# One split, one chain and one decay block in another order, and a second buffer for the end-decay exponent, in the HGRN2 mixer of a two-block model

## The reference, cut to what matters

```python
def hgrn2_scan(q, k, v, logf, s0, with_output):
    ...
    kc, vc = chunks(k), chunks(v)
    gcum = jnp.cumsum(chunks(logf), axis=2)
    g_end = gcum[:, :, -1]
    k_end = kc * jnp.exp(g_end[:, :, None] - gcum)
    chunk_states = jnp.einsum("bcshk,bcshv->bchkv", k_end, vc)
    s_final, s_in = lax.scan(_carry_step, s0, (jnp.moveaxis(jnp.exp(g_end)[..., None], 1, 0),
                                               jnp.moveaxis(chunk_states, 1, 0)))
    ...
    q_rel = qc * jnp.exp(gcum - g_mid)
    k_rel = kc * jnp.exp(g_mid - gcum)
    att = jnp.where(causal, jnp.einsum("bclhk,bcshk->bchls", q_rel, k_rel), 0.0)
    o_intra = jnp.einsum("bchls,bcshv->bclhv", att, vc)
    o_inter = jnp.einsum("bclhk,bchkv->bclhv", qc * jnp.exp(gcum), s_in)
    return (o_intra + o_inter).reshape(bsz, seqlen, nh, dv), s_final
```

## Time and profile before

| what | value |
|---|---|
| median of three runs | 2863.11 us |
| profiled execution, its own time | 2866.0 us |
| its span | 2863.2 us |
| PE busy | 2325.6 us (81%) |
| DVE busy | 1724.7 us (60%) |
| ACT busy | 1282.8 us (45%) |
| rounds 1 and 2 and what leads in, 2163 to 2224 us | 61.0 us |
| rounds 3 to 8, 2224 to 2388 us | 164.0 us |

### The profile page before, as it was taken

How to read it: one execution, slowest core, us unless ns; L and a number is a source line. 1 busy time by engine, 2 the same in 40 slices (tenths; PEclk the granted TensorE clock), 3 DMA queues, 4 the chain that set the end, 5 groups by cost and what they waited for, 6 DMA issues and landing times. The chain is left out here.

```text
span 2863.2 us, 36429 instructions
## 1 busy us (share of the span) xinstructions
PE 2325.6 (81%) x11964; PEld 1845.0 (64%) x11964; DVE 1724.7 (60%) x2894; ACT 1282.8 (45%) x1924; POOL 254.2 (9%) x329
## 2 busy tenths in 40 slices
PE   4999799899878787776766977999658886689994
PEld 3989666789841565655663446778547776577783
DVE  4773425376310348997884026999645877379994
ACT  2663125365210345543112025888536663168883
POOL 0000000000000055652000000111100000001100
PEclk8999899899999798987887987999879898789997
DMA  5344321344359421210000216999812111289992
GB/s 190 147 170 150 119 95 38 114 165 162 122 220 409 163 67 59 66 55 20 1 1 0 74 73 220 390 389 391 312 52 82 60 59 45 75 310 396 395 395 102
DMA packets 126952, 454.75 MB, mean 159 GB/s; under 512 B 13792, under 2 KB 17504, under 8 KB 126688
## 3 DMA queue, kind: packets, MB, share of 16 engines
q1 hardware_dynamic: 115872, 413.15, 38.9%
q0 software_dynamic: 10944, 39.85, 3.7%
HBM read 431.97 MB, written 20.97 MB: 158 GB/s over the span
## 5 line engine op out<-in xcount | busy, mean ns | idle before, releaser
L2136 DVE TENSOR_TENSOR moe_w_lo<-ring,moe_w_hi 128x1024 fp32r<-128x1024 f32 x384 | 462.5, 1221 | 62.3 <-ACT moe_w_hi L2074 57.2
L2074 ACT CAST moe_w_hi<-ring 128x1024 fp32r<-128x1024 f32 x384 | 399.2, 1049 | 147.4 <-PE ps L252 119.6
L250 PE MATMUL ps<-ffn_h_hi,ffn_w_hi 128*128 128x256 f32 x704 | 205.4, 292 | 33.0 <-DVE ffn_h_lo L369 17.3
L250 PE MATMUL ps<-moe_w_hi,moe_own 128*128 128x512 f32 x512 | 213.9, 418 | 12.0 <-DVE moe_own L2143 11.1
L251 PE MATMUL ps<-moe_w_lo,moe_own 128*128 128x512 f32 x512 | 205.0, 400 | 0.0
L252 PE MATMUL ps<-moe_w_hi,moe_own 128*128 128x512 f32 x512 | 204.8, 400 | 0.0
L251 PE MATMUL ps<-ffn_h_lo,ffn_w_hi 128*128 128x256 f32 x704 | 202.1, 287 | 0.0
L252 PE MATMUL ps<-ffn_h_hi,ffn_w_lo 128*128 128x256 f32 x704 | 202.0, 287 | 0.0
L250 PE MATMUL ps<-even_h_hi,even_w_hi 128*128 128x512 f32 x320 | 140.0, 438 | 74.9 <-DVE even_w_lo L1403 74.7
L359 DVE TENSOR_TENSOR ffn_w_lo<-ring,ffn_w_hi 128x1024 fp32r<-128x1024 f32 x132 | 155.3, 1218 | 68.4 <-ACT ffn_w_hi L326 68.4
L326 ACT CAST ffn_w_hi<-ring 128x1024 fp32r<-128x1024 f32 x132 | 131.3, 1046 | 125.7 <-PE ps L252 69.0
(11 more groups left out here) (426 smaller groups left out, 5468.7 us busy)
## 6 DMA issues: line engine op xcount, KB each, us to landing
ring<-in_weights SPq DMA_DIRECT2D x766, 512.0 KB, 5.7
expert_rows<-moe_y POOLq DMA_DIRECT2D x32, 512.0 KB, 7.2
token_rows<-moe_token_rows SPq DMA_DIRECT2D x6, 512.0 KB, 2.6
sq<-in_cmp_w SPq DMA_DIRECT2D x1, 2048.0 KB, 7.9
both<-in_x SPq DMA_DIRECT2D x1, 1024.0 KB, 5.9
both<-in_context SPq DMA_DIRECT2D x1, 1024.0 KB, 8.2
out<-both SPq DMA_DIRECT2D x1, 1024.0 KB, 4.8
cols<-in_cols SPq DMA_DIRECT2D x1, 724.5 KB, 9.3
```

Of the source, the lines that this page charges most:

```text
L250: pe.matmul(out, w_hi, x_hi, start=start, stop=False)
L2074: act.copy(w_hi[:, j % WB].rearrange("p h f -> p (h f)"), k.slot(act, first + GU + j, e).rearrange("p a f -> p (a f)")).then_inc(w_rounded, 1)
L2136: dve.tensor_tensor(w_lo[:, j % WB].rearrange("p h f -> p (h f)"), k.ring[:, (first + GU + j) % RING].rearrange("p a f -> p (a f)"), w_hi[ ...
```

## The change

In `exps` the first exponential reads `ke[:, d, :]` and not `logs[:, d, :]`, and in `decays` the difference "end of chunk minus running sum" is written into `ke[:, d, :]`. Since PE's transposes of the head before read `ke`, `decays` waits for them (`turned`, from head 1 on). On ACT, the cast at place 0 stands ahead of `exps(h-1,0)`. On DVE, `chain(h-2,0)` stands behind the split at place 0, and `decays(h-1,1)` behind that chain.

```diff
@@ exps
-                        act.activation(ke[:, d, :], logs[:, d, :], ACT.Exp)
+                        act.activation(ke[:, d, :], ke[:, d, :], ACT.Exp)
@@ ACT, for h in range(ROUNDS)
                         if live(h - 2):
                             keep_turned(h - 2, 0)
+                        for n in places[0]:
+                            split(n + WB)
                         if live(h - 1):
                             exps(h - 1, 0)
-                        for n in places[0]:
-                            split(n + WB)
                         if live(h - 2):
                             keep_turned(h - 2, 1)
@@ decays
+                        if h:
+                            dve.wait_ge(turned, u - 1)
                         if d == 0:
-                            dve.tensor_tensor(L.rearrange("p (c t) -> p c t", t=GC), end, chunks, ALU.subtract)
+                            dve.tensor_tensor(ke[:, d, :].rearrange("p (c t) -> p c t", t=GC), end, chunks, ALU.subtract)
                             mid, edge = HC // 2 - 1, HC - 1
                         else:
-                            dve.tensor_tensor(L, gg[:, :], L, ALU.subtract)
+                            dve.tensor_tensor(ke[:, d, :], gg[:, :], L, ALU.subtract)
                             dve.drain()
-                            dve.tensor_tensor(chunks, end, L.rearrange("p (c t) -> p c t", t=GC), ALU.subtract)
+                            dve.tensor_tensor(chunks, end, ke[:, d, :].rearrange("p (c t) -> p c t", t=GC), ALU.subtract)
@@ DVE, for h in range(ROUNDS)
                         if live(h - 1):
                             decays(h - 1, 0)
-                            decays(h - 1, 1)
                         if live(h - 2):
                             mask(h - 2, 0)
-                            chain(h - 2, 0)
                         for n in places[0]:
                             split(n + WB)
+                        if live(h - 2):
+                            chain(h - 2, 0)
                         if live(h - 1):
+                            decays(h - 1, 1)
                             weigh(h - 1, 0)
```

## The result

| what | before | after |
|---|---|---|
| median, first comparison (4 runs each) | 2861.27 us | 2883.85 us |
| its ratio, 95% interval | | 1.0078, 1.0052 to 1.0102 |
| repeat, later (23 and 6 runs) | 2867.01 us | 2884.33 us |
| its ratio, 95% interval | | 1.0064, 1.0051 to 1.0078 |
| span of the profiled execution | 2863.2 us | 2880.8 us |

The changed kernel is slower, as forecast, but by more: 22.6 us in the first comparison, 17.3 in the repeat, 13.7 forecast. 2883.85 us lies above the range (2867 to 2882).

What follows compares the result with a forecast made beforehand. The bound was a loop: PE from mix to attend 1, then 9.64 us over ACT and DVE to the next mix. Waits of 11.3 plus 2.4 of clock gave 13.7 us: 2876.8 us from 2863.1, range 2867 to 2882.

Steps and rivals of the forecast that it cites:

- The chain in rounds 3 to 7: DVE's cast-split-chain-decays row starts direction 1's exponential at C + 9.47 against C + 8.21: 1.26 us later a round, 6.3 in all.
- Round 8: Two tiles at place 0, attend 1 early: direction 1's exponential moves from C + 5.60 to C + 9.47, 3.87 us of delay.
- C: The start of carry 0 on PE in a round, from which the prediction counts the other starts; 2288.74 in round 5.
- Rounds 1 and 2: In round 1 a split stands ahead of the decays that `exps(0,1)` waits for; 1.14 us together, through to round 3's mix.
- Edits at nothing: Transposes' wait, direction 0's exponentials behind the cast, writing `ke`, the first exponential in place and SyncE's queue: costed at 0.
- The wait for the transposes: In round 5 DVE stands 0.7 us before decays 0 writes `ke`; idleness before the split covers it, so cost 0.
- The clock: PE's halved clock after idle gaps, from mix to C: 0 to 4.8 us more with longer gaps, half taken, 2.4.
- rival 3: The clock drop falls into the longer idle gap and is over when the mix begins: -3.1 us, 2860 us; chance 0.04.
- Rival 1: Every gap costs the full clock price, round 9's mix too: 8.0 us of clock, total 19.3, 2882 us; chance 0.20.
- Rival 2: In rounds 3 to 7 the slow clock reaches past C, attend 1 is late and hides the delay: 2868 to 2870.5 us; chance 0.11.
- Rival 4: The place 0 split no longer stands between chain 0 and `weigh`, freeing the chain: 2863 us, no change; chance 0.05.

Runs made afterwards that it cites:

- the parts: The change's three parts, each alone against the kernel before: ACT's order, ratio 1.0009; the buffer and its wait, 1.0010; DVE's order, 1.0086.
- the filled kernels: Kernel before and changed kernel with 10 and 15 overwritten matmuls in PE's gaps before the mix: ratios 0.9949 and 0.9982 to the unfilled kernel before.

## Why the prediction was right in its mechanism and wrong in its size

1. *The chain in rounds 3 to 7.* Right: 1.29 us a round against 1.26, link by link, and the exponential changed its releaser. By the parts, DVE's order makes it, not the cast and not the buffer.
2. *Round 8.* Right: 3.89 against 3.87 us, C + 9.49, and the round grew to 32.5 us, not the 29.3 that the prediction asked for, since 3.2 us of clock came on top (13.12 us from mix to carry 0 for 9.89).
3. *Rounds 1 and 2.* 1.14 forecast, 1.3 and 2.0 measured, 2.6 between the filled kernels. That without the early cast DVE's order would have cost another 6 us here was not seen: the cast had been costed at nothing.
4. *Edits at nothing.* The wait for the transposes held DVE for 1.2 to 1.7 us, not 0.7, because the mix and turn 0 took 0.9 us longer at the low clock; the idleness ahead of the split covered it, as was said.
5. *The clock: the step that failed.* The prediction took 3.2 us as the full price of a gap, gave each stretch at most that, and took the half of 4.8 us. The term was 5.9 and 5.5 us, above even its upper end, and single stretches lost up to 4.4 us. 3.2 was only about the largest loss that gaps of 3.0 us showed. Windows of round 5 (two) and round 7 of the kernel before, cut where the clock changes (the third number from the end is the granted clock):

```profile
2278.53:2279.50 0.97, 0.97 (x9) 0.97 (x10) 0.97 (x2) 0.97 (x2) 0.00 (x0) 1.00 0.00 0
2279.50:2286.33 6.83, 6.83 (x34) 6.83 (x34) 6.53 (x13) 3.68 (x6) 0.00 (x0) 0.50 0.22 77
...
2334.11:2334.69 0.58, 0.00 (x0) 0.03 (x1) 0.51 (x3) 0.57 (x2) 0.00 (x0) 0.50 0.00 0
```

and of round 6 of the changed kernel, the end of the gap and the way from the mix on:

```profile
2308.87:2309.82 0.95, 0.00 (x0) 0.03 (x1) 0.71 (x3) 0.94 (x2) 0.00 (x0) 0.50 0.21 82
2309.82:2319.11 9.29, 9.29 (x44) 9.29 (x45) 7.34 (x14) 3.79 (x6) 0.00 (x0) 0.50 0.17 59
```

Before, the mix of round 5 began at full clock, and 6.8 us of the way to carry 0 ran at half. In the changed kernel the clock had fallen 0.95 us ahead of the mix, and 9.3 us ran at half: 11.4 us for 7.0. The clock was back 2.4 and 2.1 us ahead of carry 0, so the low stretch grew at both ends. That none of the drops of before lay in a gap, as the prediction says against rival 3, is a misreading: in round 7 the clock fell 0.58 us ahead of the mix. The two kernels with the repeated mask show that a longer gap is enough to raise the loss; why the clock then stays low for longer is not shown. Of the prediction's two readings, losses drawn anew (0) and a longer gap that makes the drop surer (4.8), the second is nearer, but both are at work: round 3, with the same gap of 3.0 us in all three, lost 3.2 us before, 1.6 changed and 0 in the repeat. With the means of the table, which only the later runs gave, the five lengthened gaps of rounds 4 to 8 would have cost 1.5 us more each (3.8 - 2.3), 7.5 in all, and the forecast would have been 2882 us.
6. *The rivals.* Rival 1's 19.3 us lies between the two comparisons (22.6 and 17.3), but with the wrong terms: it had 8.0 us of clock, of which 5.9 came, and round 9's mix stayed fast. Rival 2 did not occur: the clock was back ahead of C. Of rival 3 only the beginning is right: part of the low clock falls into the gap, 0.95 us in round 6, but the longer gap costs more and not less. Rival 4 fell with the part kernels.

The first comparison's 22.6 us is 5 more than the 17.5 seen in the mixer. The changed kernel reads 2883.85 and 2884.33 us in the two comparisons; the kernel before reads 2861.27 in the first (4 runs) and 2867.0, 2867.7 and 2867.4 us in the three later ones (23, 17 and 9 runs). So these 5 us come mostly from a lower reading of before, and why it was lower stays open. Without them, the 3.8 us by which the terms were short (3.5 of them the clock's) lead from 2876.8 to 2880.6 us, inside the range.

## What to carry to other kernels

Before an instruction is moved behind another in an engine's queue, write down what each of the two is waiting for: here the decays went behind a split that waits, over ACT, for PE, and 7.6 us of slack became 1.3 us of delay a round. Where PE idles in a loop, price the waits and the clock apart, and do not take the loss after one length of gap as the ceiling for a longer one. The better move was to take the work that ends a round (mask and chain) out from behind the work that only the next round needs.

## What was not expected of the hardware

The loss to the clock grows with the gap and then stays, in the mean: 2.3 us after gaps of about 3.0 us, 3.8 after 4.2 to 4.6, 3.5 after 6.3 to 6.6. In a round of 28.1 us before it was 3.2 us, half of the round's excess over the 22 us that PE is busy at full clock (21.9 with mask and chain moved), and 2.3 us of useless matmuls in each gap of 3.0 us returned all of it (14.3 us in six rounds).
